# A Hymba layer on one core: input sums made by accumulating transfers, and another order of the vector, scalar and matrix work around the first pair of Strassen products

## What is computed

```python
proj = h @ w_in
gq, gk, gv, g_lr, g_gate, hq, hf, hi, h_gate = jnp.split(proj, IN_OFFSETS, axis=-1)
...
scores = jnp.where(causal, jnp.einsum('bhncd,bhnsd->bhncs', q_rel, k_rel), 0.0)
o_intra = jnp.einsum('bhncs,bhnse->bhnce', scores, v)
chunk_update = jnp.einsum('bhncd,bhnce->bhnde', k_to_end, v)
...
o_hgrn = merge_heads(rms_norm(o_hgrn, hgrn_norm_g)).astype(h.dtype) * jax.nn.silu(h_gate)
return jnp.concatenate([o_gla, o_hgrn], axis=-1) @ w_out
```

## Time and profile before

| what | value |
|---|---|
| runs of the kernel | 1164.38, 1164.15, 1166.89 us |
| median | 1164.38 us |
| the profiled execution, its own time | 1166.44 us |
| its span in the profile | 1164.7 us (1.7 us lie around it) |
| TensorE | busy 1137.4 us, 98%; 89% of the chain that ended last |
| VectorE, ScalarE, GpSimd | busy 876.3, 612.9, 499.4 us (75%, 53%, 43%) |
| mean granted clock of TensorE | 0.993 of 2.4 GHz |
| waits of TensorE, longest groups | 4.4 us for the first x, 3.8 in six for sq_lo, 1.9 and 0.8 for pw_lo |

### The profile page before, as it was taken

One profiled execution on the slowest core, in us unless ns is written; L12 is line 12 of the kernel. 1 busy time (PEld: TensorE's weight loads), 2 busy tenths in 40 slices (PEclk: granted clock), 3 DMA queues, 4 the chain that ended last, 5 costly groups with the idle time before them and its releaser, 6 DMA issues.

```text
span 1164.7 us, 15675 instructions
## 1 busy us (share of the span) xinstructions
PE 1137.4 (98%) x5555; PEld 939.3 (81%) x5555; DVE 876.3 (75%) x1048; ACT 612.9 (53%) x933; POOL 499.4 (43%) x318
## 2 busy tenths in 40 slices
PE   7999999899999999999999999999999999999996
PEld 6788788787878787888888888888888888788885
DVE  6898888877777677477976765677795884966776
ACT  7763564756566566345654555455664433424424
POOL 1021111534243344427534353344466675666741
PEclk9999999999999999999999999999999999999999
DMA  9777353044353549421455344544624637447203
GB/s 359 259 235 271 128 175 97 1 127 129 93 177 98 154 123 295 143 93 73 137 170 181 136 155 135 181 144 157 194 64 159 223 91 264 147 132 279 72 1 145
DMA packets 160549, 180.44 MB, mean 155 GB/s; under 512 B 7508, under 2 KB 119256, under 8 KB 157784
## 3 DMA queue, kind: packets, MB, share of 16 engines
q1 hardware_dynamic: 160472, 179.44, 46.4%
HBM read 138.51 MB, written 40.89 MB: 154 GB/s over the span
## 4 chain that ended last, share of the span: by engine, by line
PE 89%; DVE 4%; DMA 2%; ACT 2%; issue 1%; SPq 1%; POOL 1%; DVEq 0%; ACTq 0%
PE unit_bank L1742 16%; PE unit_bank L2156 9%; PE unit_bank L2158 9%; PE unit_bank L2157 9%; PE small_bank L2156 9%; PE small_bank L2158 9%; PE small_bank L2157 9%; PE unit_bank L2003 3%; PE small_bank L1742 3%; PE unit_bank L2005 3%; PE unit_bank L2004 3%; PE small_bank L1879 2%; DVE ada_acc L2257 1%; PE small_bank L1781 1%; DMA ada_slot<-in_w_ada_dram 1%
## 5 line engine op out<-in xcount | busy, mean ns | idle before, releaser
L997 POOL TENSOR_TENSOR wr_lo<-quarter,wr_hi 128x512 fp32r<-128x512 f32 x122 | 197.6, 1632 | 174.4 <-ACT wr_hi L1530 174.3
L2156 PE MATMUL unit_bank<-op_hi,wr_hi 128*128 128x512 f32 x452 | 176.5, 390 | 1.1 <-issue 1.1
L2158 PE MATMUL unit_bank<-op_hi,wr_lo 128*128 128x512 f32 x452 | 175.9, 389 | 0.0
L2157 PE MATMUL unit_bank<-op_lo,wr_hi 128*128 128x512 f32 x452 | 175.9, 389 | 0.0
L2156 PE MATMUL small_bank<-op_hi,wr_hi 128*128 128x512 f32 x448 | 174.5, 390 | 0.0
L2158 PE MATMUL small_bank<-op_hi,wr_lo 128*128 128x512 f32 x448 | 174.3, 389 | 0.0
L2157 PE MATMUL small_bank<-op_lo,wr_hi 128*128 128x512 f32 x448 | 174.3, 389 | 0.0
L1530 ACT ACTIVATE wr_hi<-wr_full 128x512 fp32r<-128x512 f32 x90 | 56.8, 631 | 173.3 <-DVE wr_full L2903 173.3
L2903 DVE TENSOR_TENSOR wr_full<-quarter,quarter 128x512 f32<-128x512 f32 x90 | 88.9, 989 | 56.3 <-PE small_bank L2158 23.0
L1530 ACT ACTIVATE wr_hi<-quarter 128x512 fp32r<-128x512 f32 x136 | 83.0, 626 | 90.5 <-PE unit_bank L2158 48.4
L1742 PE MATMUL unit_bank<-a_hi,w_hi 128*128 128x512 f32 x304 | 121.2, 399 | 0.8 <-DVE w_lo L2401 0.8
(11 more groups left out here) (366 smaller groups left out, 2397.2 us busy)
## 6 DMA issues: line engine op xcount, KB each, us to landing
quarter<-in_w_mlp_dram SPq DMA_DIRECT2D x128, 256.0 KB, 4.1
hidden_scratch<-hid SPq DMA_DIRECT2D x98, 256.0 KB, 2.4
ada_slot<-in_w_ada_dram SPq DMA_DIRECT2D x48, 512.0 KB, 6.1
op_full<-hidden_scratch SPq DMA_DIRECT2D x21, 1024.0 KB, 4.8
pair_quarter<-in_w_in_dram SPq DMA_DIRECT2D x32, 256.0 KB, 3.7
piece_x<-t_scratch SPq DMA_DIRECT2D x16, 512.0 KB, 4.1
piece_y<-t_scratch SPq DMA_DIRECT2D x32, 256.0 KB, 3.3
raw<-in_w_out_dram SPq DMA_DIRECT2D x16, 512.0 KB, 4.5
```

Of the source, the lines that this page charges most:

```text
L997: pool.tensor_tensor(wr_lo[slot][:, :, :], split_source(n), wr_hi[slot][:, :, :].bitcast(F32), ALU.subtract).then_inc(wr_lo_pool, 1)
L2156: pe.matmul(dst, wh, ah, start=opens, stop=False, skip_group_check=True)
L2157: pe.matmul(dst, wh, al, start=False, stop=False, skip_group_check=True)
L2158: mm = pe.matmul(dst, wl, ah, start=False, stop=k == KH - 1, skip_group_check=True)
```

## The change

Three of the four sums of inputs are no longer made by VectorE. VectorE still makes a01 (xs1), a11 (now xs2) and T3, with the other sign, xs2 + xs1. GpSimd then issues six transfers of 1 MB, each waiting for the one before: a_hi and a_lo of a00 are added into xs1 by accumulating transfers (after w_lo of unit 9), xs1 into xs2 and xs2 copied to xs3 (after that of unit 11; the copy also waits until t3 is stored), and a_hi and a_lo of a10 into xs3 (after unit 12). So xs1, xs2 and xs3 are T1, T2 and T4, with other signs than before, and the weight sums S1, S2, S4 and two joins change signs to match; S2 becomes one scalar_tensor_tensor of the same size.

T1's high part is made on ScalarE after the second read-out of H0 (before: after the norm's exponentials); its low part goes from GpSimd (four operations) to VectorE (`low_first_sum`, one operation), where T2 was made. S2 moves ahead of the decay and q_cum. In the first pair (early == 0) ScalarE does the logarithms, keys, the copy of the first part, the exponentials, P6's and P5's weights, and T4's high part, in this order; VectorE does S1, a join, the norms, states, masks, T4's low part, S4, and the first head's gate last; TensorE does P6 directly behind "up", with pieces 1 and 2 of P7 after P5 and piece 3 after P4. On SyncE the four loads of x are put between the loads of output weights.

```diff
+            def add_into(n, dst, src):
+                if n:
+                    pool.wait_ge(sums_added, 16 * n)
+                pool.dma_start(dst[:, :, :], src, accum_op=ALU.add).then_inc(sums_added, 16)
...
             for u in range(2, U_OUT):
                 low(u, u % 2)
-            pool.wait_ge(t_high, T_HIGH_0 + 2)
-            for k in range(KH):
-                ins = pool.tensor_tensor(t1_lo[:, k, :], xs[1][:, k, :], t1_hi[:, k, :].bitcast(F32), ALU.subtract)
-            ins.then_inc(pair_lo, 1)
+                if u == 9:
+                    pool.wait_ge(split_hi, 16)
+                    pool.wait_ge(lo_dve, 16)
+                    pool.wait_ge(t_made, T_MADE_0 + 3)
+                    add_into(0, xs[1], part_of(a_hi, 0, 0))
+                    add_into(1, xs[1], part_of(a_lo, 0, 0))
+                if u == 11:
+                    add_into(2, xs[2], xs[1][:, :, :])
+                    pool.wait_ge(t3_stored, T3_STORED_0 + 32)
+                    pool.wait_ge(sums_added, 48)
+                    pool.dma_start(xs[3][:, :, :], xs[2][:, :, :]).then_inc(sums_added, 16)
+            add_into(4, xs[3], part_of(a_hi, 1, 0))
+            add_into(5, xs[3], part_of(a_lo, 1, 0))
...
+            def low_first_sum():
+                dve.wait_ge(t_high, T_HIGH_0 + 2)
+                dve.wait_ge(sums_added, 48)
+                dve.tensor_tensor(t1_lo[:, :, :], xs[1][:, :, :], t1_hi[:, :, :].bitcast(F32), ALU.subtract).then_inc(t_made, 1)
...
-                pair_high(early, P6)
-                wait_join(act, early, 0)
-                keys(0)
-                copy_part(early, 0)
-                pair_high(early, P5)
+                if early:
...
+                else:
+                    first_logs()
+                    keys(0)
+                    copy_part(early, 0)
+                    first_exps()
+                    pair_high(early, P6)
+                    pair_high(early, P5)
+                    fourth_high()
...
                 pair_product(early, P6)
+                if early:
+                    seventh_piece(early, 2)
+                attend(2)
+                pair_product(early, P5)
                 if not early:
                     seventh_piece(early, 1)
-                seventh_piece(early, 2)
-                attend(2)
-                pair_product(early, P5)
-                seventh_piece(early, 3)
+                    seventh_piece(early, 2)
+                else:
+                    seventh_piece(early, 3)
                 attend(3)
                 pair_product(early, P4)
+                if not early:
+                    seventh_piece(early, 3)
...
-            for i in range(2):
-                load_x_back(i)
-            for v in range(2, 4):
+            load_x_back(0, 0)
+            load_out(2)
+            load_x_back(1, 0)
+            for v in range(3, OUT_HALVES):
                 load_out(v)
-            sp.wait_ge(normed, before("ss", 7))
-            sp.wait_ge(seventh_done, SEVENTH_0 + 4 * PAIRS)
-            for i in range(4):
-                for pr in range(2):
-                    load_quarter(0, pr, i)
-            for v in range(4, OUT_HALVES):
-                load_out(v)
+                if v in (5, 6):
+                    load_x_back(v - 5, 1)
+                if v == 7:
+                    sp.wait_ge(normed, before("ss", 7))
+                    sp.wait_ge(seventh_done, SEVENTH_0 + 4 * PAIRS)
+                    for i in range(4):
+                        for pr in range(2):
+                            load_quarter(0, pr, i)
```

More of the change, by code:

```diff
@@ L1301, in group, with first_logs, first_exps, fourth_high @@
                     read_out(7, "v")
-                    read_out(7, "ss")
-                    act.wait_ge(t_done, T_DONE_0 + 1)
-                    act.wait_ge(t_made, T_MADE_0 + 9)
-                    act.activation(t4_hi[:, :, :], xs[2][:, :, :], ACT.Copy).then_inc(t_high, 1)
+            def first_logs():
+                for which in range(2):
+                    act.wait_ge(filled["ss"], before("ss", 2) + 2 + which + 1)
+                    act.activation(stat[:, which, :], SB[2 + which][:, :], ACT.Ln, bias=eps, scale=1.0 / P
+                                   ).then_inc(read["ss"], 1)
+            def first_exps():
+                for which in range(2):
+                    act.wait_ge(read["ss"], before("ss", 2) + 2 + which + 1)
+                    act.activation(stat[:, which, :], stat[:, which, :], ACT.Exp, scale=-0.5).then_inc(o_rms, 1)
+            def fourth_high():
+                act.wait_ge(t_done, T_DONE_0 + 1)
+                act.wait_ge(sums_added, 96)
+                act.activation(t4_hi[:, :, :], xs[3][:, :, :], ACT.Copy).then_inc(t_high, 1)
             def pair_high(p, prod):
@@ L2502, in both_read @@
                         dve.wait_ge(unit_read[half], u + 1)
-                def gate(u, n, head, half=None, place=None):
-                    th, xx = (t0[:, :], t1[:, :]) if half is None else (tok(t0, place), tok(t1, place))
-                    for hf in (0, 1) if half is None else (half,):
-                        dve.wait_ge(unit_read[hf], u + 1)
-                    dve.scalar_tensor_tensor(th, th, 1.0, xx, ALU.add, ALU.mult).then_inc(gate_silu, 1)
-                    dve.wait_ge(gate_silu, n + 1)
-                    dve.wait_ge(normed, before("ss", gi) + (half + 1 if half is not None and head == 7 else 0))
-                    dst = row(mixed, head) if half is None else tok(row(mixed, head), half)
-                    dve.scalar_tensor_tensor(dst, th, 0.5, dst, ALU.mult, ALU.mult).then_inc(gated, 1)
                 u0 = 4 * gi + 1
@@ L2590, in group, with first_norms, first_gate @@
                     low_third()
-                if own == "H":
-                    weight_sum_of(0, "S2")
-                    add_parts(xs[2], 1, 0, 7)
-                    subtract(xs[2], xs[2], xs[3], 8)
-                read_out(7)
+                if own == "P":
+                    read_out(7)
                 if name == "P0":
                     then(dve.memset(masked[:, :, :], 0.0))
-                if own == "H":
-                    gate(u0 + 3, hh, hh)
+            def first_norms():
+                for which in range(2):
+                    dve.wait_ge(o_rms, before("ss", 2) + 2 + which + 1)
+                    dst = tok(mixed[:, 2 + which], 1)
+                    dve.scalar_tensor_tensor(dst, dst, cols[:, R_GG:R_GG + 1], stat[:, which, :], ALU.mult, ALU.mult
+                                             ).then_inc(normed, 1)
+            def first_gate():
+                for half in range(2):
+                    dve.wait_ge(unit_read[half], 13)
+                dve.scalar_tensor_tensor(t0[:, :], t0[:, :], 1.0, t1[:, :], ALU.add, ALU.mult).then_inc(gate_silu, 1)
+                dve.wait_ge(gate_silu, 1)
+                dve.wait_ge(normed, before("ss", 2))
+                dve.scalar_tensor_tensor(mixed[:, 0], t0[:, :], 0.5, mixed[:, 0], ALU.mult, ALU.mult).then_inc(gated, 1)
             def weight_sum_of(p, kind):
```

81 lines of the change are left out of this document (46 added, 35 removed).

## The result

The changed kernel takes 1168.85 us (median of 14 runs, 1167.27 to 1172.47); the kernel before takes 1165.76 us (14 runs, 1164.15 to 1166.89). The ratio is 1.0031, with a 95% interval of 1.0023 to 1.0038: 2.7 to 4.4 us slower. The prediction was 1163.4, between 1160.4 and 1168.0, so the time lies outside its range. It is 0.31% slower, just past the 0.3% from which the prediction speaks of slower, and to that it gave a chance of 0.14. Its base was off too: the median of three runs, 1164.38, is 1.4 us under that of fourteen.

The account below looks back on a forecast made before the run. TensorE, busy 98% of the span, was taken as the bound, so only its waits and lower clock count. -2.8 + 2.56 - 0.8 = -1.0 us gave 1163.4 against the median 1164.38, range 1160.4 to 1168.0.

Parts of the forecast that it names:

- Step 1: First pair after H0: TensorE's waits before P7 and P2 both go, -2.68 us, and P2 runs at full clock.
- Step 2: First pair: P6 starts near 236.0 instead of 238.79, -2.8 us, after TensorE stands 2.5 to 3 us.
- Step 3: Lower clock behind the wait before P6: P6 loses what P2 lost, +2.56 us, bounds 0 and 2.8.
- Step 4: First pair: P7's pieces 1 and 2, and 3, behind P5 and P4, and the first head's gate last, cost nothing.
- Steps 5 and 6: T1's rounding on ScalarE and low part on VectorE; six 1 MB transfers at 8.8 us each, limit 13.8: nothing.
- rival of slow transfers: Transfers over 13.8 us delay T1's low part on VectorE: 1166.9 at 15 us, 1175.9 at 18; chance 0.14.
- Step 7: SyncE's queue at projection's end: weight's load ahead of three x loads ends TensorE's 0.8 us wait; -0.8, other end 0.
- the rivals: Clock holds, chance 0.2; slow transfers, 0.14; P7's low part ahead of q_cum, 0.1; P2's wait stays, 0.04.

Follow-up runs that it names:

- P6 first: Changed kernel with P6's weight rounded on ScalarE ahead of the first pair's logarithms, keys, copy and exponentials: 1164.33 us, ratio 0.9981.
- the gate alone: Changed kernel with the first head's gate moved ahead of the masks on VectorE, nothing else: 1168.15 us, ratio 1.0019.
- the old loads: Changed kernel with SyncE's loads of x, output weights and quarters at the projection's end in their old order: 1169.14 us, ratio 1.0035.
- the quarters first: Changed kernel with three second-pair weight-quarter loads ahead of piece 3's load, and S4 ahead of masks and T4's low part: 1167.01 us, ratio 1.0008.
- the pieces alone: Kernel before with only P7's pieces 1 and 2 behind P5 and piece 3 behind P4 in the first pair: 1170.51 us, ratio 1.0039.
- the squares first: Changed kernel with P6's weight, quarters and S4 first, plus first-pair output and squares ahead of P7's weight, sq_lo ahead of the forget gate: 1163.59 us.
- the pieces put back: Changed kernel with P7's pieces 1 and 2 behind P6 and piece 3 behind P5 again in the first pair: 1166.24 us, ratio 1.0001.

## Why the prediction was wrong, by its own steps

- **Step 1 was right.** The waits at P7 and P2 went, and P2 ran in 2.92 us (230.96 to 233.88).
- **Step 2 was right.** P6 started at 238.30, which is 235.93 without the 2.37 us of the early part, for 236.0 forecast. The stop was 3.26 us where 2.5 to 3 were forecast, since P2 started, and "up" ended, sooner than forecast (235.04, or 232.67 without the early part, for 233.5 at most). The run with P6 first shows that the stop and the lower clock behind it were on the path: 4.5 us went with them.
- **Step 3 was right.** The lower clock came. In this execution it came only 1.5 us after P6 had begun (L2049 at 239.79) and cost 1.62 us up to P3, not 2.56; behind the same stop the way from P6 to P3 was longer than before by 1.60 us in the run with the gate alone, 2.62 with the old loads and 2.85 with the quarters first. The forecast lies inside that scatter.
- **Step 4 failed: "They are the same matmuls; nothing else reads them before the join of that quarter ... Nothing."** The engine's own work was looked at, not what waits for its end. The end of piece 1 releases a load in SyncE's queue with two quarters behind it, and the end of piece 3 releases VectorE's join and the place that S3 is written to. Both lead over ScalarE to the squares. Put at nothing, the step was a stop 3.3 us longer and 2.51 us of lower clock; the pieces alone, in the kernel before, were 4.6 us. The same step put the gate at nothing too, "without that cover it would cost its two passes behind the masks": that cost was mostly hidden behind the late pieces, and came out as 1.4 us when they were put back. With both taken back the kernel is 1.5 us faster than before, near the -1.0 that the rest of the sum gives.
- **Steps 5 and 6 were right in what came of them.** T1's low part started at 194.91, as soon as the masks ahead of it on VectorE were done. The five accumulating transfers took 7.6 to 10.4 us and the copy 6.3, for 8.8 assumed and a limit of 13.8. The rival of slow transfers fell with that. The limit itself was reckoned on the wrong path: the third transfer did not start when the second had landed but behind the low part of unit 11, at 182.28, which left it 12.6 us up to 194.91; that this is close to 13.8 is luck. The profile's list of DMA issues after (medians of two; the last row is one accumulation and the copy):

```profile
x_sum<-a_hi POOLq DMA_DIRECT2D x2, 1024.0 KB, 9.7
x_sum<-a_lo POOLq DMA_DIRECT2D x2, 1024.0 KB, 8.9
x_sum<-x_sum POOLq DMA_DIRECT2D x2, 1024.0 KB, 7.6
```

- **Step 7 was right**: the wait for w_lo went, and the last stretch is 0.9 us shorter, which goes again with the old order of the loads.

So the sum was -2.8 + 2.56 - 0.8 = -1.0 and the trace reads -2.86 + 1.62 - 0.9 + 5.80 = +3.6; the one missing term, 5.80, is larger than any other. None of the rivals had it: they asked about prices and the clock, none about the queues that a moved step releases.

What stays open is whether S3 and the joins can be had earlier still. The run with the squares first suggests that this chain ends last in the second pair, but no run shortened it with P6 early; P6 first with the gate ahead of the masks was not run.

## What to carry to other kernels

When a step is moved on one engine, list first what its end releases: buffers, the loads that refill them, and whatever stands behind those loads in the same queue, on every engine. A part that seems to cost nothing (here the late gate) may only be covered by another part that is later still (the pieces): put the later one back, then price the other. And a gain on one path (P6 first, 4.5 us) can need the very part that costs on another: with P6 early the pieces' old place cost 3.72 us at piece 1.

## What the runs showed of the hardware

From issue to landing the five accumulating transfers of 1 MB took 7.6 to 10.4 us, 9.1 in the median, and the plain copy 6.3, against 4.8 us for the 1 MB load in the earlier trace rows. The third one held GpSimd at most 9.45 us: it was issued at 182.28, and GpSimd went on at 191.73. The Trainium skill, page "DMA: Bandwidth & Descriptors", section on the anatomy of the software path, gives a fit that comes to an estimate of 4.4 us; the accumulating transfers took about twice that, and the measurement decides. The stall that the Trainium skill, page "SBUF — State Buffer", section "SBUF: two separate sides", names for transfers on GpSimd's queue is not seen: none of the six took over 10.4 us, with VectorE at work beside them (tensor_tensor, scalar_tensor_tensor, a scan). The Trainium skill names it there for VectorE's two-port modes, and whether any instruction beside these transfers ran in one, no run here shows.

The clock fell at different moments behind like stops: behind 3.26 us in the changed kernel P6's first six matmuls still ran at the full clock, while in the run with the quarters first P6 ran from its first matmul at the lower one behind 3.23 us (235.50 to the scores at 240.79, 5.29 us against 4.01). Behind a stop of 1.58 us (the pieces put back) it stayed at 1.00, and behind one of 1.4 us for ada_acc it fell. At that place, near 27 us, the length of the stop does not decide: behind 0.83 us it fell (quarters first, 0.72 from 28 to 34), behind 0.91 it did not (the pieces alone, 1.00).
